# Attention stage of a hybrid trunk: projection per unit from dense copies of its tokens, transposes inside the projection, turned tiles evicted ahead of the squares

## The chip, the core and the metric

The kernel runs on one core of a Trainium2 chip. The metric is the device time in microseconds (us) of one execution; the time before is the median of three runs. The engines named below are PE (TensorE: matmuls and transposes; its weight loads are shown apart as PEld), ACT (ScalarE), DVE (VectorE), POOL (GpSimd) and SP (SyncE, which here only issues DMAs). Each takes its own instructions in the order in which they are written; between engines only semaphores order the work.

## What is computed

Two layers over 1024 tokens of width 1024 in float32. Layer 0 mixes tokens by a dilated sliding-window attention, layer 1 by an mLSTM; behind each comes a squared-ReLU MLP. The change is in the attention of layer 0 alone:

```python
def attention_mixer(x, w_in, q_gain, k_gain, w_out, rel_bias):
    qkv = (x @ w_in).reshape(b, s, 3, N_GROUPS, ATTN_HEADS, ATTN_HEAD_DIM)
    for g, (window, dilation) in enumerate(((128, 1), (512, 4), (2048, 16))):
        q = rms_norm(qkv[:, :, 0, g], q_gain[g]) * (ATTN_HEAD_DIM ** -0.5)
        k = rms_norm(qkv[:, :, 1, g], k_gain[g])
        o, l = dilated_window_attention(q, k, qkv[:, :, 2, g], rel_bias[:, g], window, dilation)
    # each query attends to positions t, t-d, ..., t-window; softmax with a bias per distance
    wts = softmax(stack(lses), axis=0)          # the three groups are merged by their denominators
    y = einsum('gbsh,gbshe->bshe', wts, stack(outs))
    return y.reshape(b, s, -1) @ w_out
```

There are 16 heads of width 64 and three groups g with window and dilation (128, 1), (512, 4) and (2048, 16). In group 1 only tokens that are equal modulo 4 meet, in group 2 only those equal modulo 16.

## The kernel before

The attention works on **sections**: one section is a pair of heads in one group, so there are 8 pairs x 3 groups = 24 sections. A section is cut into 8 **units** of 128 queries. All matmuls are float32 products made of three passes: each operand is split into a high and a low part (`_hi`, `_lo`), and `split_matmul` (L67 to L71) multiplies high by high, high by low and low by high.

One **step** (a superstep `st`, which is a section, and a tile `j` of 0 to 7) does the following, and `run_supersteps` writes the same step for every engine. Of a step's work some belongs to the tile that is projected now and some to a unit projected before.

- PE, in this order: 24 matmuls of 256 columns that project q and k of 128 tokens of this section into `ps_qk` (its weight operand is the 128 tokens of `hT_hi` or `hT_lo`); transposes of the tile before (`qkn`, L526) and of one tile of v (`vT`, L530) into `ps_t`; transposes of the probabilities of a unit (L547) into `ps_p`; 6 matmuls of 512 columns that project a quarter of the work for v over half of the tokens (`ps_v`); the scores of the next unit into `ps_s`; that unit's predecessor's product of probabilities and v into `ps_o`.
- ACT: the exponentials of a unit (L635, one for each of two heads), the copies of `ps_o` to the output buffer (L651, L652), the high part of one slice of the next section's weights (L602), the squares of the projected q and k (`sq`, L667), the high part of the turned probabilities (`pT_hi`, L673), of the turned q and k (`qk_hi`, L684, two) and of v (`v_hi`, L688). Twice in a section it copies `ps_v` into `vT`, with the tokens in the order of the group (L621, L625).
- DVE: bias and maximum of the scores (L723, two) and its negative (`neg_max`, L726); the sums of the squares (`ss`, L732) and `var` (L737); the low parts of the turned tiles (L743, L758, L764); the normalised q and k (`qkn`, L779). In some steps it also merges the three groups of a pair: short operations on 64 partitions (L794 to L823), and five over 128x1024 elements (L830, L837, L840, L844, L847).
- POOL: the low part of the weight slice (`w_lo`, L857), and `rs`, the power -1/2 of `var` (L879).

For groups 1 and 2 a unit's tokens lie apart in the sequence. The evictions put them together: `perm_view` and `perm_dest` read and write the turned tiles in the group's order. So a unit's q and k are whole only when the whole section has been turned, and the units lag a section (8 steps) behind the projection. A unit has a predecessor in its window (then its scores have 256 columns for each head and there are four transposes of probabilities and six matmuls into `ps_o`) in 7 of 8 units of group 0, in 4 of 8 of group 1 and in none of group 2; otherwise they are 128 columns, two and three. Such units are called long and short below.

What orders the work across engines at the place of the change: `qk_mm` (PE to ACT: projected), `squared` (ACT to DVE), `var_done` (to POOL), `rs_done` (back to DVE), `qkn_done` (to PE, for L526); and for the unit `scored`, `neg_done`, `exp_done` (PE to DVE to ACT to PE, for L547) and `p_turned`. Steps of the supersteps 4 to 21 stand in a loop of three rounds of six supersteps.

Of the kernel before, what the change touches and what calls it, by code (L numbers as in the profile page):

```python
# [29 lines left out]
NG = len(GROUPS)  # L30
HEADS = 16
# [17 lines left out]
def bias_onehot():  # L49

    out = np.zeros((NG, REL_BUCKETS + 1, BIAS_LEN), np.float32)
    exact = REL_BUCKETS // 2
    for g, (window, dilation) in enumerate(GROUPS):
        band = window // dilation
        for x in range(BIAS_LEN):
            step = x - (P - 1)
            if step < 0 or step > band:
                out[g, REL_BUCKETS, x] = 1.0
                continue
# [14 lines left out]
def perm_view(ap, g, width):  # L74

    if g == 0:
        return ap
    return ap.rearrange("p (i r) -> p r i", r=GROUPS[g][1])


def perm_dest(buf, g, t0, width):

    if g == 0:
        return buf[:, t0:t0 + width]
    d = GROUPS[g][1]
    if g == 1:
        n, i0 = t0 // HALF, (t0 % HALF) // d
        return buf.rearrange("p (r n i) -> p r n i", r=d, n=2)[:, :, n, i0:i0 + width // d]  # L90
    return buf.rearrange("p (r i) -> p r i", r=d)[:, :, t0 // d:(t0 + width) // d]


def natural_view(buf, g):

    if g == 0:
        return buf
    if g == 1:
        return buf.rearrange("p (r n i) -> p n i r", r=4, n=2)
    return buf.rearrange("p (r i) -> p i r", r=16)  # L100


def split_tokens(ap, g):
# [5 lines left out]
    return ap.rearrange("p (i r) -> p i r", r=16)  # L109


# [192 lines left out]
LAST_SUPER = SECTIONS + 2  # L304
# [18 lines left out]
class AttentionBuffers:  # L323


    def __init__(self, nc, ctx):
        sb = lambda n, s: ctx.enter_context(nc.sbuf_tensor(n, s, F32))
        self.vT = sb("vT", [P, 2, SEQ])
# [4 lines left out]
        self.x_tiles = [b[:, i, :] for b in (self.vT, self.o_g0, self.w_bc) for i in range(2)]  # L333
# [3 lines left out]
def attention_phase(nc, ones, ident, buffers, total, norm_gain, hT_hi, hT_lo, wqkv, q_gain, k_gain, bias_dram, yT_dram):  # L337
# [3 lines left out]
    with ExitStack() as ctx:  # L341
# [8 lines left out]
        qk_hi = sb("qk_hi", [P, 2, 2, SEQ], F32R)  # L350
        qk_lo = sb("qk_lo", [P, 2, 2, SEQ], F32R)
        v_hi = sb("v_hi", [P, 3, P], F32R)
        v_lo = sb("v_lo", [P, 3, P], F32R)
# [13 lines left out]
        vT, w_bc, prob = buffers.vT, buffers.w_bc, buffers.prob  # L367
        o_raw = [buffers.o_g0, total[:].rearrange("p (o t) -> p o t", o=1), buffers.o_g2]
        ring = sb("ring", [P, HALF])
        compact = sb("compact", [64, NG, 2, 2, 16])  # L370
        top = sb("top", [64, 2, 16])
        diff = sb("diff", [64, NG, 2, 16])
        grown = sb("grown", [64, NG, 2, 16])
        part = sb("part", [64, NG, 2, 16])
        den = sb("den", [64, 2, 16])
        share = sb("share", [64, NG, 2, 16])

        ps_qk = [ps(f"ps_qk{i}", [P, HALF]) for i in range(2)]
        ps_v = ps("ps_v", [P, HALF])
# [12 lines left out]
        qk_mm, v_mm, turned = sem("qk_mm"), sem("v_mm"), sem("turned")  # L392
# [4 lines left out]
        vT_done = sem("vT_done")  # L397
# [26 lines left out]
        def _(sp):  # L424
# [4 lines left out]
            sp.dma_start(gains[HD:P, 1, :], k_gain).then_inc(gains_in, 16)  # L429
            for n in range(TT + 4):  # L430
# [4 lines left out]
            def step(i, st, j):  # L435
# [1468 lines left out]
```

## Time and profile before

| | |
|---|---|
| median of 3 runs | 3385.18 us (3384.01 to 3385.2) |
| the profiled execution | 3383.74 us |
| its span, first to last instruction | 3382.0 us |
| busy: PE, PEld, DVE, ACT, POOL | 94%, 79%, 39%, 33%, 24% of the span |
| mean granted clock of PE | 0.978 of full speed |
| HBM traffic over the span | 51 GB/s |

The profiler took one execution. Busy time says how much an engine had to do; what sets the time is which engine the others wait for. Matmuls overlap in the profile: one of 256 columns is shown as 0.28 us long while the next starts 0.12 us behind it, so for PE the distance from start to start is what counts. The attention's projections start at 35 us and the last one starts at 1262 us; the output projection starts at 1332 us. The rest of the span is the MLPs and the mLSTM.

### The profile page before, as it was taken

The page shows a single profiled execution, that of the slowest core. Times are in us where ns is not written, and L with a number is a line of the kernel's source. Part 1 is how long each engine was busy: PE and PEld are TensorE (multiplying, and loading weights), DVE is VectorE, ACT ScalarE, POOL GpSimd, SP SyncE. Part 2 cuts the span into 40 slices and gives each one's busy share as a digit, 9 for nine tenths or more (in the row PEclk, how much of TensorE's full clock was granted, in tenths as well). Part 3 has the DMA queues.
Part 4 walks back from the last instruction along what each step waited for, and adds up shares of the span by engine and source line. Part 5 has one row for each costly group of instructions (what it writes and reads, how often), then busy time and mean ns, then how long its engine had stood idle before and what let it go on. Part 6 is the DMA issues. An engine that isn't in the chain of part 4 may idle for free. (4 is left out here: it accounts for less than half of the span.)

```text
span 3382.0 us, 48256 instructions
## 1 busy us (share of the span) xinstructions
PE 3192.3 (94%) x17466; PEld 2669.5 (79%) x17466; DVE 1334.0 (39%) x3725; ACT 1102.1 (33%) x3002; POOL 825.2 (24%) x598
## 2 busy tenths in 40 slices
PE   4999999999999995999999999899877999999999
PEld 3888888888888883878888888678655788888887
DVE  6445454555555554341313133541064431313131
ACT  4555555555555553321111112210244211111020
POOL 3332333333233320212222122112111122222221
PEclk9999999999999995999999999999998999999999
DMA  2112121211112114111111111111201111111112
GB/s 98 36 40 59 41 58 40 61 49 50 52 45 53 47 32 150 50 44 47 48 50 44 50 50 45 38 44 50 81 26 57 44 50 44 50 50 44 50 45 80
DMA packets 89904, 177.01 MB, mean 52 GB/s; under 512 B 25515, under 2 KB 55870, under 8 KB 89662
## 3 DMA queue, kind: packets, MB, share of 16 engines
q1 hardware_dynamic: 87358, 169.63, 16.1%
q10 hardware_dynamic: 2304, 4.20, 0.3%
q8 instruction: 147, 2.41, 0.3%
q14 instruction: 95, 0.78, 0.1%
HBM read 160.67 MB, written 13.12 MB: 51 GB/s over the span
## 5 line engine op out<-in xcount | busy, mean ns | idle before, releaser
L69 PE MATMUL ps_qk<-w_hi,attn_hT_hi 128*128 128x256 f32 x1536 | 437.4, 285 | 23.3 <-DVE attn_hT_lo L213 9.7
L915 POOL TENSOR_TENSOR first_w_lo<-first_raw,first_w_hi 128x1024 fp32r<-128x1024 f32 x96 | 231.7, 2414 | 900.8 <-ACT first_w_hi L911 900.8
L70 PE MATMUL ps_qk<-w_lo,attn_hT_hi 128*128 128x256 f32 x1536 | 436.1, 284 | 0.0
L71 PE MATMUL ps_qk<-w_hi,attn_hT_lo 128*128 128x256 f32 x1536 | 436.1, 284 | 0.0
L857 POOL TENSOR_TENSOR w_lo<-raw,w_hi 128x384 fp32r<-128x384 f32 x192 | 194.6, 1015 | 701.9 <-ACT w_hi L602 701.9
L915 POOL TENSOR_TENSOR second_w_lo<-second_raw,second_w_hi 128x1024 fp32r<-128x1024 f32 x72 | 172.2, 2391 | 630.0 <-ACT second_w_hi L911 630.0
L69 PEld LDWEIGHTS ps_qk<-w_hi,attn_hT_hi 128*128 128x128 f32 x1536 | 294.1, 191 | 27.6 <-issue 13.3
L635 ACT ACTIVATE prob<-ps_s,neg_max 128x128 f32<-128x128 f32 (+1 forms) x384 | 156.6, 413 | 439.7 <-DVE neg_max L726 439.7
L70 PEld LDWEIGHTS ps_qk<-w_lo,attn_hT_hi 128*128 128x128 f32 x1536 | 294.7, 192 | 0.4
L71 PEld LDWEIGHTS ps_qk<-w_hi,attn_hT_lo 128*128 128x128 f32 x1536 | 294.9, 192 | 0.0
L69 PE MATMUL first_ps<-first_hid_hi,first_w_hi 128*128 128x512 f32 x640 | 255.4, 399 | 32.7 <-DVE first_hid_lo L1239 32.7
L732 DVE TENSOR_REDUCE ss<-sq 128x4 f32<-128x256 f32 x192 | 80.7, 420 | 506.9 <-ACT sq L667 506.9
L69 PE MATMUL first_ps<-first_hT_hi,first_w_hi 128*128 128x512 f32 x640 | 252.6, 395 | 14.2 <-POOL first_w_lo L915 14.2
L69 PE MATMUL second_ps<-second_hid_hi,second_w_hi 128*128 128x512 f32 x640 | 251.0, 392 | 12.5 <-DVE second_hid_lo L1242 12.5
L70 PE MATMUL first_ps<-first_hid_lo,first_w_hi 128*128 128x512 f32 x640 | 254.9, 398 | 0.0
L71 PE MATMUL first_ps<-first_hid_hi,first_w_lo 128*128 128x512 f32 x640 | 254.7, 398 | 0.0
L70 PE MATMUL first_ps<-first_hT_lo,first_w_hi 128*128 128x512 f32 x640 | 251.4, 393 | 0.0
L71 PE MATMUL first_ps<-first_hT_hi,first_w_lo 128*128 128x512 f32 x640 | 251.4, 393 | 0.0
L70 PE MATMUL second_ps<-second_hid_lo,second_w_hi 128*128 128x512 f32 x640 | 250.5, 391 | 0.0
L71 PE MATMUL second_ps<-second_hid_hi,second_w_lo 128*128 128x512 f32 x640 | 250.1, 391 | 0.0
L879 POOL TENSOR_TENSOR rs<-var,minus_half 128x4 f32<-128x4 f32 x192 | 193.3, 1007 | 133.5 <-DVE var L737 125.0
L911 ACT CAST first_w_hi<-first_raw 128x1024 fp32r<-128x1024 f32 x96 | 99.9, 1041 | 383.6 <-PE first_ps L71 358.5
(276 smaller groups left out, 6853.9 us busy)
## 6 DMA issues: line engine op xcount, KB each, us to landing
raw<-in_wqkv SPq DMA_DIRECT2D x192, 192.0 KB, 2.3
first_raw<-in_w SPq DMA_DIRECT2D x64, 512.0 KB, 3.4
second_raw<-in_w SPq DMA_DIRECT2D x64, 512.0 KB, 3.4
w_bc<-share_dram SPq DMA_DIRECT2D x48, 256.0 KB, 4.2
first_raw<-in_vo_pieces SPq DMA_DIRECT2D x16, 512.0 KB, 3.5
bias<-bias_dram SPq DMA_DIRECT2D x16, 256.0 KB, 3.6
yT_dram<-o_g SPq DMA_DIRECT2D x8, 512.0 KB, 3.1
first_raw<-in_attn_wo SPq DMA_DIRECT2D x8, 512.0 KB, 3.5
```

The source lines that it names most:

```text
L69: pe.matmul(out, a_hi, b_hi, start=first, stop=False)
L70: pe.matmul(out, a_hi, b_lo, start=False, stop=False)
L71: return pe.matmul(out, a_lo, b_hi, start=False, stop=last)
L635: a = act.activation(prob[:, u % 2, h, c0:2 * P], ps_s[h][:, c0:2 * P], ACT.Exp, bias=neg_max[:, sp_, h * TT + u:h * TT + u + 1], accum_ou ...
L732: dve.tensor_reduce(ss[:], sq[:].rearrange("p (h e) -> p h e", e=HD), AX.X, ALU.add)\
L857: pool.tensor_tensor(w_lo[:, par, k, :], raw[:, slot, :], w_hi[:, par, k, :].bitcast(F32), ALU.subtract).then_inc(w_lo_done, 1)
L879: pool.tensor_tensor(rs[:], var[:], minus_half[:], ALU.pow).then_inc(rs_done, 1)
L911: act.copy(self.hi[:, n % 2, :], self.raw[:, n % self.RAW, :]).then_inc(self.hi_done, 1)
L915: pool.tensor_tensor(self.lo[:, n % 2, :], self.raw[:, n % self.RAW, :], self.hi[:, n % 2, :].bitcast(F32), ALU.subtract).then_inc(self.lo ...
```

## The change

The projection is now made unit by unit, of q, k and v together: 24 matmuls of 384 columns into `ps_qkv`, in which the weight operand is the unit's 128 tokens. For group 0 these lie side by side in `hT_hi` and `hT_lo`; for groups 1 and 2 they are copied first into the dense buffers `tile_hi` (by ACT) and `tile_lo` (by POOL), one step ahead. Since q, k and v arrive in the unit's order, the buffer `vT`, its copies and its transposes go, and `qk_hi`, `qk_lo`, `v_hi` and `v_lo` are written densely, the last two straight from `ps_qkv`. A unit can follow its projection by `LAG` = 2 steps. In group 2 a unit now holds the tokens equal modulo 8, and the bias table masks the odd distances.

On PE the transposes of turned q and k and of the probabilities stand between the fifth and the sixth of the 8 parts of the projection; scores and output product stay behind it. On ACT and DVE the evictions of turned tiles stand ahead of the squares and their sums. The merging of a pair's groups comes a superstep earlier and works on 128 partitions; SP's DMAs for bias, rows and merging move with it, and their count per pair stays nearly the same.

```diff
-LAST_SUPER = SECTIONS + 2
+LAST_SUPER = SECTIONS + 1
+LAG = 2
+EARLY_TILES = 5
...
@@ PE, step
+                    for k in range(k_first, k_end):
...
+                        h_hi = tile_hi[:, j % 2, k, :] if g else hT_hi[:, k, j * P:(j + 1) * P]
+                        h_lo = tile_lo[:, j % 2, k, :] if g else hT_lo[:, k, j * P:(j + 1) * P]
+                        mm = split_matmul(pe, ps_qkv[j % 2][:, 0:W3], h_hi, h_lo,
+                                          w_hi[:, par, k, :], w_lo[:, par, k, :], k == 0, k == KT - 1)
+                    return mm
+
+                if st < SECTIONS:
+                    if st >= 1 or j >= 2:
+                        pe.wait_ge(qkn_done, T - 1)
+                        pe.wait_ge(v_lo_done, T - 1)
+                    if st % NG:
+                        pe.wait_ge(tile_hi_done, tiles_copied(i, st, j))
+                        pe.wait_ge(tile_lo_done, tiles_copied(i, st, j))
+                    project(0, EARLY_TILES)
+                if 1 <= TT * st + j <= TT * SECTIONS:
...
+                    pe.wait_ge(qkn_done, T)
+                    for a in range(2):
+                        mm = pe.transpose(ps_t[:, a * P:(a + 1) * P], qkn[:, (j - 1) % 2, a * P:(a + 1) * P], ident[:])
...
                 if has_unit(st, j, 1):
 
                     sec, u = unit(st, j, 1)
                     g = sec % NG
                     pe.wait_ge(exp_done, U)
...
                 if st < SECTIONS:
-
-                    half = j // 4
...
-                    for k in range(2 * (j % 4), 2 * (j % 4) + 2):
-                        mm = split_matmul(pe, ps_v[:], w_hi[:, par, k, 2 * P:3 * P], w_lo[:, par, k, 2 * P:3 * P],
...
+                    project(EARLY_TILES, KT).then_inc(qkv_mm, 1)
...
@@ ACT, step (behind exponentials, output copies and w_hi)
-                if st < SECTIONS:
-                    act.wait_ge(qk_mm, T + 1)
-                    if TT * st + j >= 1:
-                        act.wait_ge(reduced, T)
-                    act.activation(sq[:], ps_qk[j % 2][:, 0:2 * P], ACT.Square).then_inc(squared, 1)
...
+                turned_probabilities()
+                if 1 <= TT * st + j <= TT * SECTIONS:
+                    act.wait_ge(turned, T)
+                    sec, t = divmod(TT * st + j - 1, TT)
+                    for a in range(2):
+                        ins = act.activation(qk_hi[:, a, t * P:(t + 1) * P], ps_t[:, a * P:(a + 1) * P], ACT.Copy,
+                                             scale=gains[:, a, sec % NG:sec % NG + 1])
+                    ins.then_inc(turn_hi, 1)
+                ahead = next_tile(st, j)
+                if ahead is not None:
+                    act.wait_ge(qkv_mm, T)
+                    act.copy(tile_hi[:, (j + 1) % 2], tile_view(hT_hi, *ahead).bitcast(F32)).then_inc(tile_hi_done, 1)
+                if st < SECTIONS:
+                    act.wait_ge(qkv_mm, T + 1)
+                    if TT * st + j >= 1:
+                        act.wait_ge(reduced, T)
+                    act.activation(sq[:], ps_qkv[j % 2][:, 0:2 * P], ACT.Square).then_inc(squared, 1)
+                    act.copy(v_hi[:, j, :], ps_qkv[j % 2][:, 2 * P:W3]).then_inc(v_hi_done, 1)
...
@@ DVE, step (behind squares, var and rs)
                     dve.wait_ge(rs_done, T + 1)
+                    dve.wait_ge(v_hi_done, T + 1)
                     if TT * st + j >= 2:
                         dve.wait_ge(turned, T - 1)
...
+                    dve.tensor_tensor(v_lo[:, j, :], ps_qkv[j % 2][:, 2 * P:W3], v_hi[:, j, :].bitcast(F32), ALU.subtract)\
+                        .then_inc(v_lo_done, 1)
                 merge_step(i, st, j)
...
@@ POOL, step
+                ahead = next_tile(st, j)
+                if ahead is not None:
+
+                    pool.tensor_copy(tile_lo[:, (j + 1) % 2], tile_view(hT_lo, *ahead).bitcast(F32)).then_inc(tile_lo_done, 1)
                 if st + 1 < SECTIONS:
                     pool.wait_ge(w_hi_done, T + TT + 1)
                     lo_part(j % 4, (st + 1) % 2, j)
```

`tile_view(h, section, u)` picks the unit's 128 tokens of each of the 8 rows of tiles; their elements lie 4 apart (16 bytes) in group 1 and 8 apart (32 bytes) in group 2. `next_tile` gives the next step's tile unless that is of group 0, so 16 of the 24 steps of a pair make a copy.

**PE, the middle of a step, before** (`ps_t` takes the turned q, k and v, `ps_p` the turned probabilities; L69 to L71 are the three passes of one product):

```order
L69 MATMUL ps_qk<-w_hi,attn_hT_hi 128x256
L70 MATMUL ps_qk<-w_lo,attn_hT_hi 128x256
L71 MATMUL ps_qk<-w_hi,attn_hT_lo 128x256
L526 MATMUL ps_t<-ident,qkn 128x128 x2
L530 MATMUL ps_t<-ident,vT 128x128
L540 REGISTER_ALU
L547 MATMUL ps_p<-ident,prob 128x128 x4
L555 REGISTER_ALU
L69 MATMUL ps_v<-attn_hT_hi,w_hi 128x512
```

The projection of q and k is complete ahead of the transposes, and only v's stands behind them. The same place of the changed kernel, in a section of group 1 or 2:

```order
L73 MATMUL ps_qkv<-w_hi,tile_hi 128x384
L74 MATMUL ps_qkv<-w_lo,tile_hi 128x384
L75 MATMUL ps_qkv<-w_hi,tile_lo 128x384
L534 MATMUL ps_t<-ident,qkn 128x128 x2
L551 MATMUL ps_p<-ident,prob 128x128 x2
```

Behind these follow nine more matmuls into the same `ps_qkv` and only then the signal `qkv_mm` for the squares: the squares moved behind the transposes of the same step.

**ACT, one step, before**, from the exponentials (L635) on:

```order
L635 ACTIVATE prob,stat<-ps_s,neg_max 128x256 x2
L651 COPY o_g<-ps_o 64x128
L652 COPY o_g<-ps_o 64x128
L602 CAST w_hi<-raw 128x384
L664 REGISTER_ALU
L667 ACTIVATE sq<-ps_qk 128x256
L673 CAST pT_hi<-ps_p 128x512
L684 ACTIVATE qk_hi<-ps_t,gains 128x4x32 x2
L688 CAST v_hi<-ps_t 128x128
```

And of the changed kernel, in a section with copies:

```order
L619 ACTIVATE prob,stat<-ps_s,neg_max 128x256 x2
L635 COPY o_g<-ps_o 64x128
L636 COPY o_g<-ps_o 64x128
L594 CAST w_hi<-raw 128x384
L651 CAST pT_hi<-ps_p 128x512
L659 ACTIVATE qk_hi<-ps_t,gains 128x128 x2
L665 CAST tile_hi<-attn_hT_hi 128x1024
L667 REGISTER_ALU
L670 ACTIVATE sq<-ps_qkv 128x256
L671 CAST v_hi<-ps_qkv 128x128
```

Between the weight slice and the squares there now stand the turned tiles and the copy of 1024 elements.

**DVE, from the negative maximum (L726) to `qkn`, before:**

```order
L726 TENSOR_SCALAR neg_max<-stat 128x2
L729 REGISTER_ALU
L732 TENSOR_REDUCE ss<-sq 128x4
L737 TENSOR_SCALAR var<-ss 128x4
L743 TENSOR_TENSOR pT_lo<-ps_p,pT_hi 128x512
L758 SCALAR_TENSOR_TENSOR qk_lo<-ps_t,gains,qk_hi 128x16x8 x2
L764 TENSOR_TENSOR v_lo<-ps_t,v_hi 128x128
L779 TENSOR_TENSOR qkn<-ps_qk,rs 128x256
```

Of the changed kernel, from the turned probabilities to the maximum of the next step (the `ISA` rows):

```order
L706 TENSOR_TENSOR pT_lo<-ps_p,pT_hi 128x256
L719 SCALAR_TENSOR_TENSOR qk_lo<-ps_t,gains,qk_hi 128x128 x2
L724 REGISTER_ALU
L727 TENSOR_REDUCE ss<-sq 128x4
L732 TENSOR_SCALAR var<-ss 128x4
L739 TENSOR_TENSOR qkn<-ps_qkv,rs 128x256
L743 TENSOR_TENSOR v_lo<-ps_qkv,v_hi 128x128
L691 MEMSET held 128x1
L696 ISA ps_s,stat<-ps_s,bias 128x128
L696 ISA stat 128x1
```

Nothing stands any more between `var` and `qkn`, and `v_lo` stands between `qkn` and the next unit's maximum.

## Rows read from the trace of the kernel before

**Rows 1.** The page's first part: busy us, share of span, instructions of each engine.
```profile
PE 3192.3 (94%) x17466; PEld 2669.5 (79%) x17466; DVE 1334.0 (39%) x3725; ACT 1102.1 (33%) x3002; POOL 825.2 (24%) x598
```
**Rows 2.** PE's waits, 300 to 1200 us: total us, times, longest.
```profile
PE ps_p L547 <- ACT prob L635: 12.9, 12, 1.3
```
**Rows 3.** Timeline of PE (start, us): first matmuls of steps; turned probabilities near the end.
```profile
71.66 0.28 PE L69 MATMUL ps_qk<-w_hi,attn_hT_hi 128*128 128x256 f32 x1
...
76.14 0.28 PE L69 MATMUL ps_qk<-w_hi,attn_hT_hi 128*128 128x256 f32 x1
...
241.90 0.29 PE L69 MATMUL ps_qk<-w_hi,attn_hT_hi 128*128 128x256 f32 x1
...
394.40 0.29 PE L69 MATMUL ps_qk<-w_hi,attn_hT_hi 128*128 128x256 f32 x1
...
1295.55 0.69 PE L547 MATMUL ps_p<-ident,prob 128*128 128x128 f32 x2 [0.53 <-ACT prob L635]
...
1298.92 0.69 PE L547 MATMUL ps_p<-ident,prob 128*128 128x128 f32 x2 [0.74 <-ACT prob L635]
```
**Rows 4.** Timeline of a step with a short unit, 673 to 679 us.
```profile
673.03 0.42 DVE L779 TENSOR_TENSOR qkn<-ps_qk,rs 128x256 f32<-128x256 f32 x1
673.37 0.29 DVE L723 CUSTOM_DVE_ANT_0 ps_s<-ps_s,bias 128x128 f32<-128x128 f32 x1
...
674.22 0.37 ACT L635 ACTIVATE prob<-ps_s,neg_max 128x128 f32<-128x128 f32 x1 [1.94 <-DVE neg_max L726]
...
675.47 0.51 ACT L602 CAST w_hi<-raw 128x384 fp32r<-128x384 f32 x1
...
676.10 0.28 PE L70 MATMUL ps_qk<-w_lo,attn_hT_hi 128*128 128x256 f32 x1
676.22 0.29 PE L71 MATMUL ps_qk<-w_hi,attn_hT_lo 128*128 128x256 f32 x1
...
676.54 0.39 ACT L667 ACTIVATE sq<-ps_qk 128x256 f32<-128x256 f32 x1 [0.56 <-PE ps_qk L71]
...
677.09 0.37 ACT L673 CAST pT_hi<-ps_p 128x256 fp32r<-128x256 f32 x1 [0.16 <-PE ps_p L547]
...
677.66 1.01 POOL L879 TENSOR_TENSOR rs<-var,minus_half 128x4 f32<-128x4 f32 x1 [0.60 <-DVE var L737]
677.87 0.28 ACT L688 CAST v_hi<-ps_t 128x128 fp32r<-128x128 f32 x1
```
**Rows 5.** Timeline of a step with a long unit that waited, 629 to 635 us.
```profile
629.22 2.03 DVE L844 TENSOR_TENSOR w_bc<-w_bc,o_g 128x1024 f32<-128x1024 f32 x1
631.17 0.43 DVE L723 CUSTOM_DVE_ANT_0 ps_s<-ps_s,bias 128x256 f32<-128x256 f32 x1
...
632.28 0.47 ACT L635 ACTIVATE prob<-ps_s,neg_max 128x256 f32<-128x256 f32 x1 [3.79 <-DVE neg_max L726]
...
633.35 0.66 PE L547 MATMUL ps_p<-ident,prob 128*128 128x128 f32 x4 [1.25 <-ACT prob L635]
633.76 0.48 PE L69 MATMUL ps_v<-attn_hT_hi,w_hi 128*128 128x512 f32 x1
634.08 0.39 PE L70 MATMUL ps_v<-attn_hT_lo,w_hi 128*128 128x512 f32 x1
634.31 0.39 PE L71 MATMUL ps_v<-attn_hT_hi,w_lo 128*128 128x512 f32 x1
...
634.56 0.58 ACT L673 CAST pT_hi<-ps_p 128x512 fp32r<-128x512 f32 x1
```
**Rows 6.** Groups by line and form: count, busy us, mean ns, idle before; last a timeline row.
```profile
L911 ACT CAST first_w_hi<-first_raw 128x1024 fp32r<-128x1024 f32 x96 | 99.9, 1041 | 383.6 <-PE first_ps L71 358.5
L915 POOL TENSOR_TENSOR first_w_lo<-first_raw,first_w_hi 128x1024 fp32r<-128x1024 f32 x96 | 231.7, 2414 | 900.8 <-ACT first_w_hi L911 900.8
L840 DVE TENSOR_TENSOR o_g<-o_g,w_bc 128x1024 f32<-128x1024 f32 x7 | 8.5, 1211 | 0.0
...
581.37 0.40 DVE L814 TENSOR_TENSOR part<-grown,compact 64x32 f32<-64x32 f32 x3
```

More of the change, by code:

```diff
@@ L54, in bias_onehot @@
         band = window // dilation
+        mixed = dilation // UNIT_STRIDE[g]
         for x in range(BIAS_LEN):
-            step = x - (P - 1)
-            if step < 0 or step > band:
+            step, other = divmod(x - (P - 1), mixed)
+            if step < 0 or step > band or other:
                 out[g, REL_BUCKETS, x] = 1.0
@@ L71, in split_matmul, with tile_view @@
     return pe.matmul(out, a_lo, b_hi, start=False, stop=last)
[L74 to L91, printed above, removed]
+def tile_view(h, section, u):
+    if section % NG == 1:
+        return h[:].rearrange("p k (n i r) -> p k r n i", n=2, r=4)[:, :, u // 2, u % 2, :]
+    return h[:].rearrange("p k (m u) -> p k u m", u=TT)[:, :, u, :]
 def natural_view(buf, g):
@@ L327, in __init__ @@
         sb = lambda n, s: ctx.enter_context(nc.sbuf_tensor(n, s, F32))
-        self.vT = sb("vT", [P, 2, SEQ])
+        with ExitStack() as early:
+            self.x_first = early.enter_context(nc.sbuf_tensor("x_first", [P, 2, SEQ], F32))
+        self.tile_hi = ctx.enter_context(nc.sbuf_tensor("tile_hi", [P, 2, KT, P], F32R))
+        self.tile_lo = ctx.enter_context(nc.sbuf_tensor("tile_lo", [P, 2, KT, P], F32R))
         self.o_g0 = sb("o_g0", [P, 2, SEQ])
@@ L332, in __init__ @@
         self.prob = sb("prob", [P, 2, 2, 2 * P])
[L333 removed]
+        self.x_tiles = [b[:, i, :] for b in (self.x_first, self.o_g0, self.w_bc) for i in range(2)]
         self.x_tiles += [self.o_g2[:, 0, :], self.prob[:].rearrange("p a h k -> p (a h k)")]
@@ L366, in attention_phase @@
         stat_rows = sb("stat_rows", [4 * TT, P])
-        vT, w_bc, prob = buffers.vT, buffers.w_bc, buffers.prob
+        w_bc, prob = buffers.w_bc, buffers.prob
         o_raw = [buffers.o_g0, total[:].rearrange("p (o t) -> p o t", o=1), buffers.o_g2]
         ring = sb("ring", [P, HALF])
[L370 to L379, printed above, removed]
+        tile_hi, tile_lo = buffers.tile_hi, buffers.tile_lo
+        compact = sb("compact", [P, NG, 2, 2, TT])
+        top = sb("top", [P, 2, TT])
+        diff = sb("diff", [P, NG, 2, TT])
+        grown = sb("grown", [P, NG, 2, TT])
+        part = sb("part", [P, NG, 2, TT])
+        den = sb("den", [P, 2, TT])
+        share = sb("share", [P, NG, 2, TT])
+        ps_qkv = [ps(f"ps_qkv{i}", [P, HALF]) for i in range(2)]
         ps_t = ps("ps_t", [P, HALF])
@@ L396, in attention_phase @@
         turn_hi, turn_lo = sem("turn_hi"), sem("turn_lo")
-        vT_done = sem("vT_done")
+        tile_hi_done, tile_lo_done = sem("tile_hi_done"), sem("tile_lo_done")
+        v_hi_done, v_lo_done = sem("v_hi_done"), sem("v_lo_done")
         maxed, neg_done, exp_done = sem("maxed"), sem("neg_done"), sem("exp_done")
@@ L583, in step @@
                     g = sec % NG
-                    whole = TT * sec + u
                     pe.wait_ge(p_hi_done, U)
                     pe.wait_ge(p_lo_done, U)
+                    pe.wait_ge(v_lo_done, U)
                     if has_unit(st, j, 2):
@@ L824, in merge_step @@
                         ins.then_inc(share_done, 1)
-                    if j == 7:
-                        o0 = o_raw[0][:, ((st - 4) // NG) % 2, :]
+                if st >= 4 and (st - 4) % NG == 0:
+                    pair = (st - 4) // NG + 2 * i
+                    o0 = o_raw[0][:, ((st - 4) // NG) % 2, :]
+                    if j == 1:
                         dve.wait_ge(wbc_in[0], 64 * pair + 32)
```

266 lines of the change are left out of this document (98 added, 168 removed).

## The prediction, made before the changed kernel was run

> **What bounds the kernel now.** I read the busy shares first, then who PE waits for, then PE's timeline step by step, then the other engines inside one step. PE is busy 94% of the span [rows 1], and in 900 us of the attention it waits only 12.9 us for the exponentials [rows 2]. Three sections in a row, the 24 steps of one pair, take 394.40 - 241.90 = 152.5 us [rows 3], 6.35 us a step. So the stage is bound by PE's own work. It stays so because the long way through the other engines has a head start: the squares begin at 676.54, in the middle of a step, 0.03 us behind the end of the last q and k matmul (676.22 + 0.29) [rows 4]. They, `var`, `rs` and `qkn` run while PE still has v, scores and output product to do. Where DVE is late, it shows at once: one operation of 2.03 us ahead of the maximum moved the exponentials, and PE stood 1.25 us ahead of L547 [rows 5].
>
> **What PE saves.** Starts of 256-column matmuls are 0.12 us apart (676.10 to 676.22) [rows 4], of 512-column ones 0.23 (634.08 to 634.31) [rows 5]. For 384 columns the trace has no row: between 0.12 and 0.23, and I take the middle, 0.175, since the cost is nearly all columns. Before: 24 x 0.12 + 6 x 0.23 + one transpose of v (0.11) = 4.37 us. After: 24 x 0.175 = 4.20. That is 0.17 us a step, 33 us over 192 steps if PE stayed the bound. Its own work would be 6.35 - 0.17 = 6.2 us a step.
>
> At the end, unit-only steps come one per 1298.92 - 1295.55 = 3.37 us [rows 3]. Their number falls from 9 to 3 with the shorter lag: -20 us. The merging behind them is the same work with the same DMAs and keeps its length.
>
> **What the new order closes into a ring.** This is the term that decides. In the changed order the squares of tile T wait for the part of the projection that stands behind the transposes of probabilities. `qkn` of tile T waits for the squares, and DVE, which takes its work in order, reaches the maximum of the next unit only behind that `qkn` and `v_lo`. The exponentials wait for the maximum, and the next step's transposes of probabilities for the exponentials. So one lap of this ring fits into one step, and a step can't be shorter than the lap. Before, the squares did not stand behind those transposes, and there was no such ring.
>
> The lap, from the start of the exponentials, for a short unit, in a step that copies a tile:
> - exponentials and output copies, to the start of the weight slice: 675.47 - 674.22 = 1.25; the slice 0.51 [rows 4]
> - turned probabilities and turned q and k, 677.09 to 677.87: 0.78 [rows 4]
> - the copy `tile_hi`, 128x1024. A dense cast of that size by ACT is 1.04 [rows 6], of which about 0.10 overlaps the next: 0.94. The squares start at 3.48
> - squares to `rs`: 677.66 - 676.54 = 1.12; `rs` 1.01, and 0.03 to DVE; `qkn` to the next start 0.34 (673.03 to 673.37); `v_lo`, half as wide, about 0.20. Together 2.70 [rows 4]
> - maximum to exponentials: 674.22 - 673.37 = 0.85 [rows 4]
>
> Sum 7.03 us. A long unit has two exponentials longer by 0.10 each, turned probabilities longer by 0.21 (0.58 against 0.37), and 632.28 - 631.17 = 1.11 instead of 0.85 [rows 4, 5]: 7.71 us.
>
> In a step without a copy PE brings the squares, not ACT. From the exponentials to L547 are 633.35 - 632.28 = 1.07, to the next matmul 0.41, then nine matmuls, the first 0.09 later than the others (0.32 against 0.23 [rows 5]): 8 x 0.175 + 0.09 = 1.49, and 0.37 to the squares. That is 3.34 for a long unit, 2.91 for a short one (exponentials 0.21, two transposes 0.22 less). With 2.70 and 1.11 or 0.85 the laps are 7.15 and 6.46.
>
> A pair has, by its sections and its units' windows, 5 short steps and 3 long ones without a copy, 8 short and 8 long with one: 5 x 6.46 + 3 x 7.15 + 8 x 7.03 + 8 x 7.71 = 171.7 us.
>
> **Merging** stands on DVE between `v_lo` and the maximum, so every microsecond of it is in the ring. Per pair: three dense operations over 1024 elements (1.21, next start 1.14 later [rows 6]) and two that read with a stride (629.22 to 631.17, 1.95 [rows 5]), 7.3 us; and 15 short ones at about 0.16 (three in 0.40 [rows 6]), 2.4 us. Before, most of that was hidden. So a pair takes 181.4 us against 152.5: +28.9.
>
> **Sum with a copy at dense speed.** 23 sections, 7.67 pairs, x 28.9 = +222. In the first section the steps 3 to 7 had no unit and took 76.14 - 71.66 = 4.48 [rows 3]; now they take 6.46 + 3 x 7.15 + 7.71 = 35.6 instead of 22.4: +13. The end: -20. Together +215, on 3383.7 of the profiled execution: 3598 us.
>
> **The copy's stride.** This is the least certain price. `tile_view` reads elements 16 or 32 bytes apart in SBUF, and the trace has no such read by ACT. Lower end: the dense cast, 1.04 (less is excluded: as many elements, same engine). Upper end: what DVE needed for 1024 elements with a strided read, 2.03 [rows 5], whole. DVE's dense operation of that size took 1.21 [rows 6], so there the stride cost a factor of 1.67. I take ACT's own row times that factor, 1.72, since both read the same memory: +0.68 a copy. With 16 a pair, 127 copies: +86 us. At the upper end it is +0.98 a copy, +124 us.
>
> The Trainium skill, Advanced Engine Details and Errata, section Memory Cachelines, says that SBUF has lines of 16 bytes, that full speed needs at least two hits on a line, and that an access which takes another line for each element pays. DVE's two rows agree; it speaks against dense copies made this way. By the rule the sum has the +86 us, without it 3598 stands.
>
> POOL's copy `tile_lo` is in no ring: even at 2.41 x 1.67 = 4.0 us (its 1024-element operation [rows 6], with two inputs) plus the slice and `rs`, about 1.0 each, it is 6.0, under the lap. The weight loads are as many as matmuls and stay under a longer matmul. The extra waits of PE (`tile_hi_done`, `v_lo_done`) are met earlier in the lap. SP moves its DMAs by a superstep or less, with steps in hand.
>
> **Forecast**: 3383.7 + 215 + 86 = 3685; the median of the runs lies 1.4 above the profiled execution: 3686 us.
>
> **Rivals.**
> - *The copy runs at dense speed.* ACT reads one input where DVE reads two. Then 3598, with its own 3565 to 3640.
> - *Faster: PE stays the bound.* If DVE's maximum didn't have to stand behind `qkn`, or a lap fell under PE's own 6.2 us, PE would keep its 33 us, the end 20 and the waits of [rows 2] 13: 3318 us. For it speaks that before the change the exponentials wait idle 1.94 and even 3.79 us for their maximum [rows 4, 5], so ACT has room. Against it: the mean lap is 7.56 us, 1.3 too long, and its largest parts (`rs` 1.01, `qkn`, exponentials) have durations from rows.
> - *Copy hidden, ring by PE alone*: all steps at 6.46 and 7.15, 13 x 6.46 + 11 x 7.15 + 9.7 = 172.3 a pair, about 3530.
> - *Worse*: POOL's copy above 5.7 us enters the lap, or PE, now idle in each step, is granted half its clock for long. The latter would double its 6.2 us a step: over 900 us more. In [rows 5] PE stood 1.25 us and the next matmuls still came at 0.23.
>
> **How the numbers follow.** Strided copy, 3640 to 3750: 0.55. Dense copy: 0.30. Ring by PE alone, 3450 to 3565: 0.05. Above 3750: 0.05. Faster: 0.04, and 0.01 for no change. The range 3570 to 3750 leaves out the last four and a little of the dense case. Faster by over 0.2% 0.04, within 0.2% 0.01, slower 0.95; 0.2% is about what a measurement of this kernel can tell from no change.
>
> **What the changed profile would show.** PE: a wait ahead of the transposes of probabilities in nearly every step, released by ACT's exponentials, 1 to 2 us. Steps of 7 to 8.4 us in sections with copies, about 6.5 and 7.15 without. `tile_hi` 1.7 us, or 1.04 if I am wrong there. DVE waiting for `rs` in each step. Matmuls of 384 columns 0.175 apart. I am wrong altogether if PE's steps come at 5.7 to 6.3 us.

## The result and the profile after

The changed kernel takes **3838.39 us** (median of 4 runs, 3835.16 to 3838.98) against 3385.19 (4 runs): a ratio of 1.1335, 95% interval 1.1315 to 1.1354. The prediction was 3686 us with a range of 3570 to 3750. The direction held; the size did not: +453 us instead of +301.

The page's first part, of after, answers to [rows 1] (columns as there):

```profile
PE 3298.3 (86%) x16122; PEld 2766.2 (72%) x16122; DVE 1446.9 (38%) x3716; ACT 1320.8 (34%) x3082; POOL 1084.8 (28%) x726
```

PE has 1344 matmuls fewer and falls from 94% to 86% of a longer span. Who waits, 300 to 1250 us (total us, times, longest), answers to [rows 2]:

```profile
ACT prob L619 <- DVE neg_max L699: 444.2, 105, 6.4
...
PE ps_p L551 <- ACT prob L619: 196.0, 102, 4.7
```

PE waits for the exponentials in nearly every step, 196.0 us where it was 12.9. That is the ring of the prediction. In a section of group 0, whose steps make no copy, three turns of q and k in PE's timeline of after (start, us), answering to [rows 3]:

```profile
254.49 0.38 PE L534 MATMUL ps_t<-ident,qkn 128*128 128x128 f32 x2
...
260.96 0.38 PE L534 MATMUL ps_t<-ident,qkn 128*128 128x128 f32 x2
...
267.43 0.38 PE L534 MATMUL ps_t<-ident,qkn 128*128 128x128 f32 x2
```

The steps are 6.47 us; the prediction said 6.46. (A step is measured here and below from one start of these transposes to the next.) A step with a copy, after's timeline (ACT, DVE, POOL and PE, sorted by start), answers to [rows 4]:

```profile
220.18 2.08 POOL L832 CAST tile_lo<-attn_hT_lo 128x1024 fp32r<-128x1024 f32 x1
...
221.13 0.38 PE L534 MATMUL ps_t<-ident,qkn 128*128 128x128 f32 x2
...
221.44 0.85 DVE L699 TENSOR_SCALAR neg_max<-stat 128x2 f32<-128x2 f32 x1
222.33 0.37 ACT L619 ACTIVATE prob<-ps_s,neg_max 128x128 f32<-128x128 f32 x1 [3.69 <-DVE neg_max L699]
...
224.89 2.13 ACT L665 CAST tile_hi<-attn_hT_hi 128x1024 fp32r<-128x1024 f32 x1
226.88 0.42 ACT L670 ACTIVATE sq<-ps_qkv 128x256 f32<-128x256 f32 x1
...
228.05 1.01 POOL L841 TENSOR_TENSOR rs<-var,minus_half 128x4 f32<-128x4 f32 x1 [2.87 <-DVE var L732]
229.01 2.08 POOL L832 CAST tile_lo<-attn_hT_lo 128x1024 fp32r<-128x1024 f32 x1
229.09 0.42 DVE L739 TENSOR_TENSOR qkn<-ps_qkv,rs 128x256 f32<-128x256 f32 x1 [1.12 <-POOL rs L841]
...
229.95 0.38 PE L534 MATMUL ps_t<-ident,qkn 128*128 128x128 f32 x2
...
230.27 0.85 DVE L699 TENSOR_SCALAR neg_max<-stat 128x2 f32<-128x2 f32 x1
```

This step takes 229.95 - 221.13 = 8.82 us; the prediction had 7.03 + 0.68 = 7.71. Two rows stand out. `tile_hi` takes 2.13, not 1.72, and the squares start only behind it. And `neg_max`, an operation on 2 elements a partition, takes 0.85 us. It ends at 222.29 and 231.12; POOL's copy `tile_lo` ends at 222.26 and 231.09. The exponentials stand directly behind it.

### The profile page after: what moved, and what is told of

The parts are those of the page before. It is cut to its first block and busy times, and to the rows that moved or that the text cites. A ratio compares the mean times of both kernels' runs of the same rounds, so it can differ in the third digit from the quotient of the medians.

```text
span 3836.2 us, 46141 instructions
## 1 busy us (share of the span) xinstructions
PE 3298.3 (86%) x16122; PEld 2766.2 (72%) x16122; DVE 1446.9 (38%) x3716; ACT 1320.8 (34%) x3082; POOL 1084.8 (28%) x726
## 5 line engine op out<-in xcount | busy, mean ns | idle before, releaser
L73 PE MATMUL ps_qkv<-w_hi,tile_hi 128*128 128x384 f32 x1024 | 389.2, 380 | 49.2 <-ACT tile_hi L665 41.4
L551 PE MATMUL ps_p<-ident,prob 128*128 128x128 f32 x560 | 114.1, 316 | 334.5 <-ACT prob L619 334.5
L75 PE MATMUL ps_qkv<-w_hi,tile_lo 128*128 128x384 f32 x1024 | 370.9, 362 | 0.0
L74 PE MATMUL ps_qkv<-w_lo,tile_hi 128*128 128x384 f32 x1024 | 370.3, 362 | 0.0
L551 PEld LDWEIGHTS ps_p<-ident,prob 128*128 128x128 f32 x560 | 63.9, 152 | 380.0 <-ACT prob L619 354.0
L706 DVE TENSOR_TENSOR pT_lo<-ps_p,pT_hi 128x256 fp32r<-128x256 f32 (+1 forms) x192 | 105.0, 547 | 467.2 <-ACT pT_hi L651 467.2
L665 ACT CAST tile_hi<-attn_hT_hi 128x1024 fp32r<-128x1024 f32 x128 | 266.4, 2082 | 0.0
L832 POOL CAST tile_lo<-attn_hT_lo 128x1024 fp32r<-128x1024 f32 x128 | 264.5, 2066 | 0.0
L73 PEld LDWEIGHTS ps_qkv<-w_hi,tile_hi 128*128 128x128 f32 x1024 | 211.6, 207 | 63.1 <-ACT tile_hi L665 35.6
```

What stands on the lines that cost most here:

```text
L73: pe.matmul(out, a_hi, b_hi, start=first, stop=False)
L74: pe.matmul(out, a_hi, b_lo, start=False, stop=False)
L75: return pe.matmul(out, a_lo, b_hi, start=False, stop=last)
L551: mm = pe.transpose(ps_p[:, c:c + P], prob[:, u % 2, h, b * P:(b + 1) * P], ident[:])
L665: act.copy(tile_hi[:, (j + 1) % 2], tile_view(hT_hi, *ahead).bitcast(F32)).then_inc(tile_hi_done, 1)
L706: dve.tensor_tensor(pT_lo[:, b0:2, :], ps_p[:].rearrange("p (b c) -> p b c", b=2)[:, b0:2, :], pT_hi[:, b0:2, :].bitcast(F32), ALU.subtrac ...
```

## The experiments

The first four ran on one chip, one run each, beside before at 3388.34 us (one run); the other four on one chip beside before at 3387.35 (7 runs, 3384.1 to 3388.56), ACT's copy behind with one run and the last three with four each. So a difference of a few us between single runs says nothing. All edits are made in the changed kernel.

**No copies.** Does the ring alone cost what I said?

```diff
-                        h_hi = tile_hi[:, j % 2, k, :] if g else hT_hi[:, k, j * P:(j + 1) * P]
-                        h_lo = tile_lo[:, j % 2, k, :] if g else hT_lo[:, k, j * P:(j + 1) * P]
+                        h_hi = hT_hi[:, k, j * P:(j + 1) * P]
+                        h_lo = hT_lo[:, k, j * P:(j + 1) * P]
...
-                    act.copy(tile_hi[:, (j + 1) % 2], tile_view(hT_hi, *ahead).bitcast(F32)).then_inc(tile_hi_done, 1)
...
-                    pool.tensor_copy(tile_lo[:, (j + 1) % 2], tile_view(hT_lo, *ahead).bitcast(F32)).then_inc(tile_lo_done, 1)
```

> The changed kernel without both copies: PE reads the 128 tokens of a step straight from hT_hi and hT_lo in every section, so for groups 1 and 2 the unit holds other tokens than it should; all else, the order above all, stays. Theory A (a ring of squares, maximum and exponentials, plus the copies in it): the steps of the sections with copies fall from 8.8 and 9.1 us to the laps of the sections without, 6.46 with a short and 7.15 with a long unit, and DVE's neg_max and its five merging operations are back at 0.17, 1.2 and 2.0 us: some 3530 us. Rival B (the copies are the whole loss, there is no ring): steps of 5.7 and 6.3 us, bound by PE's own work, some 3330 us.

Measured 3548.87 us: +160.5, where the sum without copies has +145. Its waits of PE and its `neg_max` (count | total us, mean ns), 300 to 1250 us:

```profile
PE ps_p L548 <- ACT prob L616: 130.9, 115, 3.1
```
```profile
L692 DVE TENSOR_SCALAR neg_max<-stat 128x2 f32<-128x2 f32 x128 | 21.6, 169 | 4.4
```

The ring is there without any copy, at 15 us more than the prediction's sum has.

**Dense copies.** The same copies, of elements that lie side by side.

```diff
-    if section % NG == 1:
-        return h[:].rearrange("p k (n i r) -> p k r n i", n=2, r=4)[:, :, u // 2, u % 2, :]
-    return h[:].rearrange("p k (m u) -> p k u m", u=TT)[:, :, u, :]
+    return h[:, :, u * P:(u + 1) * P]
```

> The changed kernel, but both copies read 128 neighbouring tokens instead of tokens 4 or 8 apart, so for groups 1 and 2 the unit holds other tokens than it should; as many elements, the same engines and places. If the stride is what makes a copy 2.08 us long, tile_hi falls to 1.04 us and each step with a copy loses 1.0 us on ACT: 128 x 1.0 = -130 us. POOL's tile_lo gets shorter too, and then DVE's neg_max beside it waits less: up to another 46 us, and up to 40 in merging. Some 3620 to 3700 us. If length doesn't depend on stride, 3838 us stays.

Measured 3626.62 us. A short step with a copy is 7.06 us (385.58 to 392.64), against the prediction's 7.03 for a dense copy. Both copies by line and form, 300 to 1250 us, of this kernel and then of after:

```profile
L663 ACT CAST tile_hi<-attn_hT_hi 128x1024 fp32r<-128x1024 f32 x81 | 85.5, 1055 | 0.0
L830 POOL CAST tile_lo<-attn_hT_lo 128x1024 fp32r<-128x1024 f32 x82 | 85.2, 1039 | 0.0
```
```profile
L665 ACT CAST tile_hi<-attn_hT_hi 128x1024 fp32r<-128x1024 f32 x73 | 151.5, 2076 | 0.0
L832 POOL CAST tile_lo<-attn_hT_lo 128x1024 fp32r<-128x1024 f32 x73 | 150.8, 2065 | 0.0
```

The stride doubles both copies, and it costs 3838 - 3627 = 212 us. The prediction's 86 stood for ACT's copy alone; the 212 hold what POOL's longer copy does as well. In this kernel `neg_max` takes 169 ns again (the large merging operations are still slowed a little, 2.2 and 1.5 us against 1.9 and 1.2 without POOL's copy), and one step of its timeline shows why: the shorter copy is over before `neg_max` starts (385.84 against 386.06):

```profile
384.80 1.04 POOL L830 CAST tile_lo<-attn_hT_lo 128x1024 fp32r<-128x1024 f32 x1
...
386.06 0.17 DVE L697 TENSOR_SCALAR neg_max<-stat 128x2 f32<-128x2 f32 x1
```

**No copy by POOL**, ACT's kept. This prices `tile_lo`, for which the prediction had nothing.

```diff
-                        h_lo = tile_lo[:, j % 2, k, :] if g else hT_lo[:, k, j * P:(j + 1) * P]
+                        h_lo = hT_lo[:, k, j * P:(j + 1) * P]
...
-                    pool.tensor_copy(tile_lo[:, (j + 1) % 2], tile_view(hT_lo, *ahead).bitcast(F32)).then_inc(tile_lo_done, 1)
```

> The changed kernel without POOL's copy tile_lo alone; PE reads the low part straight from hT_lo (wrong tokens for groups 1 and 2), ACT's copy stays as it is. Theory A: the copy holds up DVE's neg_max (0.85 us instead of 0.17) and the five merging operations of a pair (each about 1.1 us longer) while it runs, all of which stand in the ring: -46 and -42 us and some for the short merging operations, about 3740 us, with neg_max at 0.17 and the merging operations at 1.2 and 2.0 us. ACT's copy stays at 2.0 to 2.1 us. Rival: these DVE operations are slow for another reason (ACT's copy, or the new layout): they stay at 0.85, 2.3 and 3.1 us, and the time at 3838.

Measured 3733.38 us: 105 us less than the changed kernel, although among after's waits of PE there is none for `tile_lo`. DVE's operations on SBUF alone, over the whole attention (40 to 1770 us; count | total us, mean ns), of this kernel and then of after:

```profile
L794 DVE TENSOR_TENSOR w_bc<-w_bc,total 128x1024 f32<-128x1024 f32 x8 | 15.4, 1926 | 0.6 <-DMA w_bc<-share_dram 0.6
...
L797 DVE TENSOR_TENSOR o_g<-o_g,w_bc 128x1024 f32<-128x1024 f32 x8 | 9.7, 1217 | 0.0
...
L698 DVE TENSOR_SCALAR neg_max<-stat 128x2 f32<-128x2 f32 x192 | 32.4, 169 | 6.5
```
```profile
L795 DVE TENSOR_TENSOR w_bc<-w_bc,total 128x1024 f32<-128x1024 f32 x8 | 24.1, 3010 | 0.8 <-DMA w_bc<-share_dram 0.8
...
L798 DVE TENSOR_TENSOR o_g<-o_g,w_bc 128x1024 f32<-128x1024 f32 x8 | 18.6, 2326 | 0.0
...
L699 DVE TENSOR_SCALAR neg_max<-stat 128x2 f32<-128x2 f32 x192 | 79.2, 412 | 6.6
```

`neg_max` is 79.2 - 32.4 = 47 us longer with POOL's copy. The five merging operations of a pair are two that take 1.1 to 1.3 us longer and three that take 1.1 to 1.4 longer; 5 x 1.2 x 8 pairs = 48. Both stand in the ring. That they add up to 95, close to the 105, is partly luck. Compared step by step with the same steps of the kernel without POOL's copy, the changed kernel takes:

- 35 us more in the 35 steps that hold a large merging operation, although these operations and `neg_max` are 47 us longer there. So a part of their slowing is hidden.
- 22 us more in 64 other steps in which a copy starts and its granted clock stayed at 1.00; `neg_max` is 23 us longer in them.
- 48 us more in the 37 other steps in which a copy starts and its granted clock was below 1.00; `neg_max` is only 21.5 us longer in them. Some 26 us of the 105 therefore go with PE's lower clock (see the last section), which the expectation did not have.

**POOL's copy behind its slice of the weights.** The work is the same; only the order on POOL differs.

```diff
+                if st + 1 < SECTIONS:
+                    pool.wait_ge(w_hi_done, T + TT + 1)
+                    lo_part(j % 4, (st + 1) % 2, j)
                 ahead = next_tile(st, j)
...
-                if st + 1 < SECTIONS:
-                    pool.wait_ge(w_hi_done, T + TT + 1)
-                    lo_part(j % 4, (st + 1) % 2, j)
```

> The changed kernel with one edit: POOL makes its copy tile_lo behind the low part of the weight slice instead of ahead of it, so some 3 us later in the step, beside DVE's wait for the squares instead of beside neg_max and the merging operations. Same work, all of it. Theory A: as without POOL's copy, neg_max at 0.17 and merging at 1.2 and 2.0 us, provided that rs isn't late: about 3740 us. If rs gets late behind the copy, up to 1 us a step comes back. Rival (the slow DVE operations have nothing to do with when POOL copies): 3838 us.

Measured 3744.71 us, -94. Its copy still takes 2.1 us, but between 300 and 1250 us no longer beside `neg_max`, which is back at 169 ns there (`w_bc` 1945, `o_g` 1217). PE's waits of this kernel, 300 to 1250 us:

```profile
PE ps_p L551 <- ACT prob L619: 149.5, 110, 3.2
PE ps_qkv L73 <- POOL tile_lo L835: 51.6, 56, 1.3
```

The wait for `tile_lo` is mostly not new: without POOL's copy PE waited 38.2 us at the same place for ACT's `tile_hi`. Since leaving the copy out and moving it bring nearly the same, what it cost was the moment at which it ran, not its work.

**ACT's copy behind the squares and `v_hi`**, of the tile two steps ahead (`next_tile` gets the distance as a third argument). Out of the ring's path, if the ring is what I said.

```diff
-                ahead = next_tile(st, j)
-                if ahead is not None:
-                    act.wait_ge(qkv_mm, T)
-                    act.copy(tile_hi[:, (j + 1) % 2], tile_view(hT_hi, *ahead).bitcast(F32)).then_inc(tile_hi_done, 1)
...
                     act.copy(v_hi[:, j, :], ps_qkv[j % 2][:, 2 * P:W3]).then_inc(v_hi_done, 1)
+                    second = next_tile(st, j, 2)
+                    if second is not None:
+                        act.copy(tile_hi[:, j % 2], tile_view(hT_hi, *second).bitcast(F32)).then_inc(tile_hi_done, 1)
```

> The changed kernel with one edit: ACT copies the tile of the step after the next, behind v_hi at the end of its step, instead of the next step's tile ahead of the squares. Same work, all of it. Theory A: the copy leaves the ring, since behind v_hi ACT waits for neg_max anyway; the laps are those of steps without copy, plus DVE's 0.7 us wait for POOL's copy: about 7.1 us with a short unit instead of 8.8, 7.5 with a long one instead of 9.1, so 128 x 1.65 = -210 us: about 3630 us. Rival (ACT is simply too busy): the step stays at 8.8 and 9.1, 3838 us.

Measured 3686.57 us, -152, but 57 above what I expected. `neg_max` is still held up, 300 to 1250 us:

```profile
L698 DVE TENSOR_SCALAR neg_max<-stat 128x2 f32<-128x2 f32 x117 | 48.2, 412 | 4.0
```

That was in the expectation, and where no merging comes in, the expectation holds. Steps there are 6.9 to 8.0 us. The six steps from the second of a group 2 section on take 304.4 us in pairs 2 to 8 together against 371.1 in the changed kernel: 66.7 less, where 42 x 1.65 = 69 was expected. The missing 57 us stand in the ten steps before these, in which the large merging operations and their DMAs come: 671.7 against 729.7, 58 less where 70 x 1.65 = 116 was expected. Of the five steps of a pair with a large merging operation two or three still take 9.4 to 13.4 us there, at granted clocks of 0.73 to 0.86; the copy's place on ACT does little for them.

**The maximum between `var` and `qkn`**, copies untouched. This cuts the ring: the exponentials of the next unit no longer stand behind `rs`, `qkn` and `v_lo`.

```diff
@@ DVE, step
-                if has_unit(st, j, 1):
-                    (bias, maximum and neg_max of the unit, ahead of pT_lo)
...
                     (squares' sums, var)
+                if has_unit(st, j, 0):
+                    (bias, maximum and neg_max of the next step's unit)
...
                     dve.wait_ge(rs_done, T + 1)
```

> The changed kernel with one edit: DVE makes the maximum and neg_max of the unit just scored between var and the turned tiles' successor qkn, so beside POOL's rs, instead of behind qkn and v_lo. Same work. Theory A: the lap loses rs, qkn and v_lo, and becomes squares, sums and var 1.05, maximum to exponentials 0.85 or 1.11, exponentials to squares 4.5 or 4.9 with a copy: 6.4 and 7.1 us; without a copy PE's own 5.7 and 6.3 bound. Some 3400 us, ratio to before near 1.01, and PE's waits for exponentials mostly gone. Rival (no such ring; the loss is ACT's and PE's work itself): within 50 us of 3838.

Measured 3437.79 us (4 runs, 3436.56 to 3440.26), ratio to before 1.0150, interval 1.0133 to 1.0167: -401 us by the order of one engine alone. Not all of it is the ring: the maximum has also left POOL's copy, and `neg_max` is 47 us shorter in total. PE's waits, 300 to 1250 us:

```profile
PE ps_qkv L73 <- ACT tile_hi L665: 31.1, 73, 0.7
```

The wait for the exponentials is gone from the list. Steps without a copy are 5.68 (short) and 6.34 us (long), with a copy 6.42 and 7.1: ACT's copy is still ahead of something that PE needs. `neg_max` is 170 ns, since POOL makes `rs` there and not the copy:

```profile
354.77 1.01 POOL L841 TENSOR_TENSOR rs<-var,minus_half 128x4 f32<-128x4 f32 x1 [2.30 <-DVE var L714]
355.24 0.17 DVE L731 TENSOR_SCALAR neg_max<-stat 128x2 f32<-128x2 f32 x1
```

**Both: the maximum ahead and ACT's copy behind.** The edits are the last two together.

> Both edits: ACT's copy two tiles ahead behind v_hi, and DVE's maximum ahead of qkn. Same work. Theory A: no lap is over PE's own work any more (ring: 3.3 + 1.05 + 1.1 = 5.5 us; ACT's own work with a copy 5.0 and 5.5 us), so steps of 5.7 and 6.3 us, the end 20 us shorter than before the change: 3320 to 3350 us, ratio 0.985, if DVE's merging beside POOL's copy stays hidden. Rival: over 3385 us, since some other engine's order binds (then the waits of PE name it).

Measured **3335.21 us** (4 runs, 3334.1 to 3335.61), ratio 0.9848, interval 0.9832 to 0.9865. This version beats before by 1.5%. PE's timeline and then its waits, 300 to 1250 us:

```profile
328.28 0.38 PE L534 MATMUL ps_t<-ident,qkn 128*128 128x128 f32 x2
...
333.96 0.38 PE L534 MATMUL ps_t<-ident,qkn 128*128 128x128 f32 x2
```
```profile
PE ps_o L73 <- DVE pT_lo L687: 12.8, 6, 2.2
...
PE ps_p L551 <- ACT prob L619: 1.6, 1, 1.6
```

These are steps with copies, at 5.68 us: both copies are covered, and PE is the bound again. Half of the pairs take 146.4 us, 6.10 a step, against 152.5 before the change; the others take 148 to 154. The large merging operations still take 2.3 to 3.1 us, and `pT_lo`, for which PE waits 12.8 us, stands behind them on DVE.

**The same with POOL's copy late.** `w_bc` and `o_g` in merging are still slowed in the last kernel; does moving POOL's copy, worth 94 us in the ring, bring anything outside it?

> As the run before it (both edits), and POOL's copy behind the low part of the weights. Theory A: merging operations at 1.2 and 2.0 us instead of 2.3 and 3.1, worth something only where DVE is late; but rs can now stand behind the copy in a short step of 5.7 us, and that would make qkn late. Between 3310 and 3390 us; the side on which it falls to the run before says which of the two weighs more.

Measured 3363.91 us (4 runs, 3361.57 to 3365.69), ratio 0.9933, interval 0.9916 to 0.9949: 29 us slower than without that edit. The contention is gone from merging (w_bc 2019 ns, o_g 1216), but there DVE had room for it, and it has moved to `var`: 192 of them take 56.0 us instead of 32.9. PE now starts steps late. Its waits, 300 to 1250 us, then one step of PE, POOL and DVE:

```profile
PE ps_qkv L73 <- POOL tile_lo L834: 16.9, 39, 0.8
```
```profile
335.49 2.12 POOL L834 CAST tile_lo<-attn_hT_lo 128x1024 fp32r<-128x1024 f32 x1
...
336.91 0.28 PE L75 MATMUL ps_o<-pT_hi,v_lo 128*128 128x256 f32 x1
337.05 0.59 DVE L713 TENSOR_SCALAR var<-ss 128x4 f32<-128x4 f32 x1
...
337.76 0.41 PE L73 MATMUL ps_qkv<-w_hi,tile_hi 128*128 128x384 f32 x1 [0.57 <-POOL tile_lo L834]
```

The first matmul of the projection starts at 337.76, behind the copy's end at 337.61 and 0.85 behind the matmul before it, where the run before has 0.11. `var` ends 0.03 behind the same copy. That step is 6.52 us instead of 5.68. Step by step, the 29 us lie in the steps with a copy and without a large merging operation. The steps with one are as long as before, although these operations are 46 us shorter. How much of the 29 is the late `tile_lo` (its wait is 16.9 us in that window) and how much the late `var` and `rs`, no run separates.

## Why the prediction was right in kind and too small

The runs split the loss into three terms, each a difference of two measured kernels. They add up to 450 us of the 453; the other 3 lie between the two measurements of before (3388.34 and 3385.19).

| term | forecast | measured | from |
|---|---|---|---|
| ring and merging, shorter end, no copies | +145 | +160.5 | no copies, less before |
| ACT's copy in the ring | +156 | +184.5 | no copy by POOL, less no copies |
| POOL's copy | 0 | +105 | changed kernel, less no copy by POOL |

**The ring: right.** Its laps without a copy are 6.47 short and, in the first pair, 7.16 long, against 6.46 and 7.15. In the later pairs long steps without a copy take 7.26 to 7.87, since short merging operations stand ahead of some of their maxima (0.68 us of them from 252.65 us on in the kernel without copies), which the prediction has in its merging term; the rest of that difference is not traced. That the maximum behind `qkn` and `v_lo` closes the ring is shown by moving the maximum alone, and by the kernel with both edits: with both copies in it, it takes 3335 us, 214 less than the kernel that has the ring and no copy. Of the missing 15 us at least a part is PE's clock: without copies the pairs take 173.4 to 180.0 us where the prediction has 172.3, and the longer ones hold the steps at a lower clock.

**PE's own step: right.** Matmuls of 384 columns start 0.17 to 0.18 us apart. With the ring cut and the copies covered PE's steps are 5.68 and 6.34, 6.10 on average in half of the pairs, where the prediction had 6.2, and the kernel lands at 3335, near the 3318 of the rival "PE stays the bound". That rival's condition, the maximum not behind `qkn`, was necessary and not enough: alone it gives 3438, because ACT's copy also has to leave the way to the squares.

**The end: right.** Unit-only steps are still 3.29 us (1750.64 to 1753.93) and fewer. From the start of the last projection's last matmuls to the output projection it is 45 us instead of 67, -22 where -20 was forecast.

**ACT's copy: mechanism right, size short.** The term "1.72 us", a factor of 1.67 taken from DVE's rows, measured 2.08; the factor is 2.0 (1.055 to 2.08). The upper end of the bound, 2.03 taken whole, was nearest. With it the term would be +194 against the measured +184.5, and the sum 3384 + 215 + 124 = 3723 against 3733 for the kernel without POOL's copy. A short step there is 8.1 us, by the sum 7.03 + 1.04 = 8.07. Both of the prediction's rows came from operations with two inputs, whose dense form is already slower than ACT's (1.21 against 1.04), so the factor was carried over to a shorter base. That the absolute 2.03 fits is known only afterwards: the stride added 0.8 us on DVE and 1.0 on ACT.

**POOL's copy: the step that failed.** The prediction said "POOL's copy `tile_lo` is in no ring" and looked only at whether POOL was late. POOL was not late; its copy lasts 2.07 us, half of what I allowed. But it starts behind `rs`, as `qkn` does, and so runs exactly beside DVE's way to the maximum, and `neg_max` and the large merging operations wait for it. In a short copying step at full clock it costs 0.68 us: 8.12 + 0.68 = 8.80 against 8.82 measured. That the copy costs this by the moment at which it runs is shown by three runs (no copy, 105 us less; moved, 94 less; dense copies, without the effect on `neg_max`). The prediction put this term at nothing; it measured +105, and without it 3733 would have lain in the range. Some 26 of the 105 go with the lower clock, which the prediction had only as an unlikely rival; no run sets that part alone.

The Trainium skill, SBUF — State Buffer, section SBUF: two separate sides, has this: GpSimd and DVE share a port pair as an exclusive lock for a whole instruction, which a DVE operation needs when it has two SBUF inputs or runs in a 2-port mode; who comes second is blocked. The traces agree on who waits and how long; in which mode an operation ran they do not show. `neg_max` ends 0.03 us behind POOL's copy both times above. In after's timeline a merging operation started inside a copy and took the rest of it more, 352.99 - 351.62 = 1.37, on top of its 1.93, less 0.13:

```profile
351.00 1.99 POOL L832 CAST tile_lo<-attn_hT_lo 128x1024 fp32r<-128x1024 f32 x1
```
```profile
351.42 0.28 DVE L743 TENSOR_TENSOR v_lo<-ps_qkv,v_hi 128x128 fp32r<-128x128 f32 x1
351.62 3.17 DVE L795 TENSOR_TENSOR w_bc<-w_bc,total 128x1024 f32<-128x1024 f32 x1
```

`v_lo`, which has one input in PSUM, started inside the same copy and took 0.28; `qkn`, with one in PSUM too, takes 0.42 beside the copy at 229.01, as it did before [rows 4]. The blocking goes the other way too. In the kernel with both edits POOL's `w_lo` started inside a merging operation and took 2.47 us instead of 1.01; it ended 0.88 behind that operation's end (290.98 + 3.31 = 294.29):

```profile
290.98 3.31 DVE L801 TENSOR_TENSOR w_bc<-w_bc,o_g 128x1024 f32<-128x1024 f32 x1
292.70 2.47 POOL L814 TENSOR_TENSOR w_lo<-raw,w_hi 128x384 fp32r<-128x384 f32 x1 [0.30 <-ACT w_hi L594]
```

The prediction asked only who waits for the result of POOL's new instruction, not what it keeps from running.

**The rivals.** "Dense copy" (3598) measured 3627 as an experiment, inside its range, but the copy is not dense. "Ring by PE alone" (3530) is the kernel without copies, 3549. "Worse" named a clock at half speed for long stretches. It came in part: 59 of 191 steps of the changed kernel, 649 us together, had a mean granted clock below 0.95, against 22 steps without POOL's copy and 11 without copies.

## What to carry to other kernels

When code is reordered, write down for each engine which instruction now stands behind which, and close the circle: if the output of step T comes back in order to a queue that step T+1 needs, the lap's length bounds the step, however idle the engines are. To get out of it move the one operation that needs none of the lap (here the maximum, -401 us with what it saved in blocking) and put bulk copies behind the operation that others wait for. For each new instruction on POOL ask what DVE does on SBUF at that moment, even where nobody waits for the result; and before moving it look at what it will stand beside and who needs it next: once the ring was cut, the same move put it beside `var` and made PE wait for it, and lost 29 us.

## What the hardware showed that I had not expected

- A read at 16 or 32 bytes from element to element doubles a 128x1024 cast in fp32: ACT 1.055 to 2.08 us, POOL 1.04 to 2.07. The two strides cost nearly alike: 2.05 us at 16 bytes and 2.12 or 2.10 at 32, in the changed kernel.
- A 2-element DVE operation can last 0.85 us instead of 0.17, because POOL is inside a copy (0.17 again with the copy left out or moved).
- PE's granted clock fell in many steps in which PE had stood. Of after, three steps (us, busy us of PE, PEld, DVE, ACT, POOL with counts, granted clock, DMA share, GB/s):

```profile
351.80:365.25 13.45, 8.74 (x44) 7.92 (x43) 7.83 (x15) 5.43 (x13) 5.18 (x4) 0.75 0.08 17
861.41:870.66 9.25, 7.39 (x39) 6.62 (x38) 4.08 (x17) 5.02 (x13) 4.54 (x4) 0.82 0.14 25
1074.21:1083.04 8.83, 6.14 (x38) 5.37 (x37) 3.63 (x14) 5.08 (x13) 4.07 (x4) 1.00 0.13 25
```

 The first holds a merging operation; 0.75 is a mixture of the levels 1.2 and 2.4 GHz. In it PE stood 4.71 us ahead of the transposes of probabilities. Behind that, matmuls of 384 columns started 0.32 apart; at 362.61 they were 0.18 apart again:

```profile
356.89 1.12 PE L551 MATMUL ps_p<-ident,prob 128*128 128x128 f32 x4 [4.71 <-ACT prob L619]
...
358.12 0.52 PE L74 MATMUL ps_qkv<-w_lo,tile_hi 128*128 128x384 f32 x1
358.44 0.52 PE L75 MATMUL ps_qkv<-w_hi,tile_lo 128*128 128x384 f32 x1
...
362.61 0.34 PE L73 MATMUL ps_qkv<-w_hi,tile_hi 128*128 128x384 f32 x1
362.79 0.34 PE L74 MATMUL ps_qkv<-w_lo,tile_hi 128*128 128x384 f32 x1
```

 The length of the wait alone does not decide. The second and third row are the same step of two pairs, with the same work and the same wait of 1.86 us ahead of the transposes of probabilities, once at 0.82 and 9.25 us, once at 1.00 and 8.83. In the kernel without copies, one merging step (323.27 to 332.59 us and its likes in pairs 2 to 8) had a wait of 2.8 to 2.9 us each time. Four times it took 9.32 or 9.33 us at 1.00, three times 10.82, 12.05 and 10.76 us at 0.84, 0.72 and 0.84. Why the clock fell in some and not in others stays open. Where it fell, the wait cost more than itself, and the same 16122 matmuls keep PE busy for 3298 us in the changed kernel and 3151 in the fastest.
